# Router and experts of a two-layer transformer: select products ahead of the overflow loop, a shorter overflow body, one more pass in the experts' loop, and extra matmuls while tokens are routed

## The chip, the core and the metric

The kernel runs on one NeuronCore of a Trainium2 chip. The core has a matrix engine (TensorE, PE in the rows), a vector engine (VectorE, DVE), a scalar engine (ScalarE, ACT), GpSimd (POOL) and SyncE (SP). They run their own instruction streams and wait for each other on semaphores. Weights and tokens come from device memory by DMA. The metric is the device time of one execution in microseconds, the median over the runs.

## What is computed

Four layers work on 512 rows of width 1024, in float32. The first two (`hybrid_layer`) are attention layers of three kinds. The last two (`second_block`, DEPTH = 2) are an attention followed by a mixture of 32 experts, and the change is all in the latter. In its first layer 256 context rows are carried along, so 768 rows are routed there and 512 in its second:

```python
p_grp = softmax(h @ w_group + b_group); grp = argmax(p_grp)       # 4 groups
lg = (h @ w_router + b_router)[grp]                               # 8 experts of that group
p_in, e_in = top_k(softmax(lg), 2)                                # 2 experts for each row
wts = p_top * p_in / sum(p_in)
y   = (silu(xe @ w_gate[e]) * (xe @ w_up[e])) @ w_down[e]         # for each expert e and its rows xe
out = segment_sum(y * wts)                                        # rows back in order
x   = x + gt_f * out
```

## The kernel before

A plan written in Python (`make_plan`) makes one list of steps. Each engine walks the same list and issues its own part of each step, so the order on an engine is the order of the list. TR, SC and PJ are the three pairs of PSUM banks; `tr_free`, `sc_free` and `pj_free` count their releases and `tr_full`, `sc_full` and `pj_full` their results.

**Routing.** Behind the attention each tile t of 128 rows (six in the first of the two layers, four in the second) goes through `wo` (L1020, output projection), `fin_turn` (eight transposes, L1015), `scored` (L1161, router products), `logits` (L1167), `ranks` (L1172, L1178; position of each row within its expert) and `slots` (L1184, row numbers of each expert's slots). VectorE finds the two experts of each row in between. GpSimd then gathers the rows of an expert (at most CAP = 96) by an indirect DMA, and `turn_x` (L1236) transposes them.

**Experts.** For expert r, `gate_up` and `gate_up_rest` (L1250, L1260) make the two products of the hidden layer; SiLU and copy (`hidden`, ScalarE) and the product of both (VectorE) give the hidden rows; `turn_hidden` (L1270) transposes them; `down` (L1283, L1291) makes the output rows, which VectorE writes to YR (`rows`). `step(r)` is in this order: gate_up(r+1), turn_hidden(r), gate_up_rest(r+1), turn_x(r+2), down(r). Step 0 stands alone, steps 1 to 28 are a hardware loop (L1321) of 14 passes with two steps in a pass, and steps 29, 30 and 31 are written out behind it.

**The last two experts.** The output rows of experts 0 to 29 go to memory, and those that a tile needs are gathered back (`gather_near`) and added by VectorE (`near_sum`). For the last two experts and the first tiles (NEAR = 2 tiles in the first layer, 4 in the second) the rows stay on the core: `select(t, g)` (L1030) multiplies a selection matrix SLOTTOK[g] (transposed at L1333) with YR[g], for g = 0, 1, into bank t of SC. VectorE adds the bank to the tile in the step `combine`, and `combine_end` normalises it.

**The overflow loop.** An expert with over 96 rows has its further rows worked out in a loop over groups of three blocks (OVER_GROUP), five groups in the first layer and four in the second. On every engine it reads a count, and each pass begins with a test of it:

```python
count = pe.value_load(OVI[0:1, MAX_OVER:MAX_OVER + 1], ...)   # L1348
with pe.Fori(0, over_groups(s.l)) as i:                       # L1349
    with pe.If(j < count):                                    # L1351, passes over the body
        for b in range(OVER_GROUP):                           # L1353, written out three times
```

No weights are loaded for it in the profiled execution: the page has 34 + 30 loads of a gate matrix, which are the 2 x 32 experts, so the body is passed over each time.

**Order around it.** TensorE issues select(0, 0), goes through the loop, and issues the remaining select products in the steps `combine`. VectorE does near_sum of tile 0, the rows of expert 31, near_sum of tile 1, then its own loop, and then the combine steps. Behind the first layer, `fin_turn` of tile 0 and the projection of the next layer (`qkv`, L1201) follow on TensorE; the projection of tile t waits until ScalarE has copied the transposed rows, and in the middle of it the next tile is transposed.

## Time and profile before

| | us |
|---|---|
| runs | 2999.82, 2997.36, 2999.81; median 2999.81 |
| profiled execution | 3009.7 |
| its span (first to last instruction) | 3008.0 |
| TensorE busy in the span | 2817.6 (94%) |
| VectorE, ScalarE, GpSimd busy | 1143.6, 749.9, 324.0 |
| mean granted TensorE clock | 0.968 of full |

The profile is one execution. A matmul of float32 operands is two MATMUL records, each with a weight load (LDWEIGHTS); a transpose is one of each. In a timeline row the number in brackets is the idle time of the engine in front of the row, and the name behind it is what ended that idle time. "issue" is idle time of an engine in which it waited for nothing that the profile names. PEldq and DVEq are the sequencers of TensorE and VectorE, which also run the branches.

### The profile page before, as it was taken

What the parts mean: (1) busy time and instruction counts of PE and PEld (TensorE: products, weight loads), DVE (VectorE), ACT (ScalarE), POOL (GpSimd) and SP (SyncE); (2) the same over time, 40 slices, a digit from 0 to 9 for tenths busy, and PEclk for the clock granted to TensorE, in tenths of its full rate; (3) what the DMA queues carried; (4) which work ended last, traced back from release to release, by engine and by line L of the source; (5) the groups of instructions that cost most, each with busy time, mean ns of one, the idle gap of its engine ahead of it and who ended that gap; (6) DMA issues with size and microseconds to landing.
All of it is one profiled execution on the core that took longest, in us unless ns stands there. A gap on an engine that the chain in (4) does not pass through costs nothing. (4 is left out here: it accounts for less than half of the span.)

```text
span 3008.0 us, 64877 instructions
## 1 busy us (share of the span) xinstructions
PE 2817.6 (94%) x27041; PEld 1647.7 (55%) x27041; DVE 1143.6 (38%) x2779; ACT 749.9 (25%) x1580; POOL 324.0 (11%) x580
## 2 busy tenths in 40 slices
PE   8999999999889999998999999879999799999994
PEld 4444655444654456545666666534565566666662
DVE  2572753572744245454112211353443522112213
ACT  1111531111542156511111111142664111111111
POOL 2000520000520000011100010120000100100001
PEclk9999999999989999998999999989999899999997
DMA  7112643212743100346999999941003699999992
GB/s 267 68 56 84 236 149 105 74 56 84 248 149 124 56 2 2 128 160 254 398 398 403 403 402 395 348 145 64 1 2 120 238 389 402 402 397 405 402 363 84
DMA packets 155293, 636.36 MB, mean 212 GB/s; under 512 B 19712, under 2 KB 24320, under 8 KB 138736
## 3 DMA queue, kind: packets, MB, share of 16 engines
q1 hardware_dynamic: 114624, 517.59, 44.4%
q0 software_dynamic: 40496, 116.39, 11.3%
q8 instruction: 118, 1.93, 0.3%
q14 instruction: 55, 0.45, 0.0%
HBM read 581.91 MB, written 52.00 MB: 211 GB/s over the span
## 5 line engine op out<-in xcount | busy, mean ns | idle before, releaser
L1052 PE MATMUL PJ<-WR,XT 128*128 128x512 f32 (+2 forms) x1152 | 478.0, 571 | 5.7 <-ACT XT L140 3.3
L140 ACT ACTIVATE PT<-TR 128x512 f32<-128x512 f32 (+3 forms) x384 | 178.0, 494 | 904.4 <-PE TR L1270 734.8
L1052 PEld LDWEIGHTS PJ<-WR,XT 128*128 128x128 f32 x1152 | 216.7, 192 | 245.8 <-issue 218.6
L140 DVE TENSOR_TENSOR PR<-G 128x384 f32<-128x384 f32 x64 | 35.7, 558 | 745.3 <-ACT G L140 744.8
L1020 PE MATMUL PJ<-WR,XT 128*128 128x512 f32 x576 | 258.5, 605 | 1.8 <-ACT XT L140 1.4
L1250 PE MATMUL SC<-QK,XT 128*64 128x256 f32 x2112 | 243.5, 384 | 0.0
L140 DVE TENSOR_REDUCE SM<-SC 128x1 f32<-128x768 f32 (+6 forms) x208 | 173.7, 835 | 169.6 <-PE SC L1093 163.0
L1201 PE MATMUL PJ<-WR,XT 128*128 128x512 f32 x512 | 228.7, 599 | 6.1 <-issue 6.1
L1250 PE MATMUL SC<-WR,XT 128*64 128x256 f32 x1984 | 226.2, 381 | 0.0
L1093 PE MATMUL SC<-QK 64*128 64x512 f32 (+7 forms) x512 | 189.3, 534 | 10.8 <-ACT PR L140 10.8
L1250 PEld LDWEIGHTS SC<-QK,XT 128*64 128x64 f32 x2112 | 149.9, 138 | 85.9 <-issue 15.3
L140 ACT ACTIVATE PR<-SC,SM 128x256 f32<-128x256 f32 (+5 forms) x288 | 187.8, 670 | 34.8 <-DVE SM L140 25.6
L1250 PEld LDWEIGHTS SC<-WR,XT 128*64 128x64 f32 x1984 | 139.8, 137 | 79.6 <-issue 12.3
L1020 PEld LDWEIGHTS PJ<-WR,XT 128*128 128x128 f32 x576 | 109.7, 194 | 132.4 <-issue 130.2
L140 ACT ACTIVATE XT<-TR 128x384 f32<-128x384 f32 (+1 forms) x200 | 98.1, 528 | 334.5 <-PE TR L1236 233.8
L1116 PE MATMUL PJ<-V,PT 128*64 128x65 f32 (+1 forms) x3904 | 169.4, 233 | 0.9 <-DVE XS L140 0.8
L1201 PEld LDWEIGHTS PJ<-WR,XT 128*128 128x128 f32 x512 | 95.9, 193 | 114.4 <-issue 114.4
L1106 PE MATMUL TR<-KF,PR 128*128 128x128 f32 x976 | 150.0, 283 | 8.5 <-DVE PR L140 7.8
L1116 PEld LDWEIGHTS PJ<-V,PT 128*64 128x64 f32 x3904 | 137.1, 138 | 36.2 <-issue 34.7
L140 ACT ACTIVATE QK<-TR 128x512 f32<-128x512 f32 (+4 forms) x100 | 54.5, 561 | 380.5 <-PE TR L1060 274.0
L1106 PEld LDWEIGHTS TR<-KF,PR 128*128 128x128 f32 x976 | 106.5, 143 | 66.4 <-ACT PR L140 46.0
L2651 POOL DMA_DIRECT2D y_rows<-XT x62 | 33.3, 537 | 957.0 <-DVE XT L140 951.1
(243 smaller groups left out, 3349.0 us busy)
## 6 DMA issues: line engine op xcount, KB each, us to landing
QK<-in_w_gate_dram SPq DMA_DIRECT2D x34, 2048.0 KB, 9.6
WR<-in_w_down_dram SPq DMA_DIRECT2D x34, 2048.0 KB, 15.8
QK<-in_w_up_dram SPq DMA_DIRECT2D x32, 2048.0 KB, 14.5
WR<-in_w_up_dram SPq DMA_DIRECT2D x32, 2048.0 KB, 14.5
WR<-in_w_gate_dram SPq DMA_DIRECT2D x30, 2048.0 KB, 9.6
QK<-in_w_down_dram SPq DMA_DIRECT2D x30, 2048.0 KB, 16.0
WR<-in_w_ada_dram SPq DMA_DIRECT2D x24, 2048.0 KB, 7.9
WR<-in_w_in_dram SPq DMA_DIRECT2D x14, 2048.0 KB, 7.7
```

What stands on the lines that cost most here:

```text
L140: return lambda *a, **k: Signal(make(*a, **k), self)
L1020: m = mm(dst[:, 0:n], rows[:, c, :], w[:, c, 0:n], start=c == 0, stop=c == DC - 1)
L1052: m = mm(bank[:, 0:n], XT1[:, c, s.t * P:(s.t + 1) * P], w[:, c, 0:n], start=c == 0, stop=c == DC - 1)
L1093: m = mm(SC[:, u.sc % 2, col:col + n], lhsT, rhs, start=all(p[0] // 512 != bank for p in ps[:k]), stop=all(p[0] // 512 != bank for p in ps ...
L1106: m = turn(bank[:, b * P:(b + 1) * P], src, identF)
L1116: m = mm(bank[r:r + HALF_ROWS, col:col + n], PT[:, o + r:o + r + HALF_ROWS], v, start=b == 0, stop=b == len(vs) - 1)
L1201: m = mm(bank, rows[:, c, :], w[:, c, :], start=c == 0, stop=c == DC - 1)
L1250: mm(bank[CAP_A * h:CAP_A * (h + 1), k * 512:k * 512 + 256], XET[par][:, c, 0:CAP_A], w[:, c, 256 * h:256 * (h + 1)], start=c == 0, stop=c ...
L2651: dma(dst, YR[r % 2][0:CAP]).then_inc(y_stored[r % 2], 16)
```

## The change

It has four parts.

1. `select` of tiles 0 and 1 is issued wholly ahead of the overflow loop; the loop's own products now go to PJ, since SC holds the results. VectorE's near_sum of tile 1 moves from ahead of its loop to behind the combine of tile 0 (in the first layer its first operation, `choices_sum`, directly behind that).
2. In the overflow loop the three blocks of a group are a hardware loop on all engines in place of three copies of the body.
3. The experts' loop takes 15 passes in place of 14 on TensorE and ScalarE. Steps 29 and 30 are in it; only turn_hidden(31) and down(31) stand behind it, with the transposes of the selection matrices between them. A loop pass also transposes expert r + 2, so there is now a gather and a turn_x for a 33rd "expert" (the index column of the first overflow block), whose rows nobody reads.
4. A new step `busy(count)` issues `count` products of the identity with a constant matrix of 512 columns into a bank of PJ, with no reader. There are 2 + 1 + 3 + 6 = 12 of them in the routing of each layer, and 2 behind the first `fin_turn` of the first layer.

```diff
@@ make_plan: routing of the last tiles
         t = moe_tiles - 1
+        def busy(count, s=None):
+            add("busy", count=count, pj=n["pj"], s=s)
+        busy(2)
         route_step("logits", t - 1)
+        busy(1)
         add("fin_turn", f=fins[t], tr=take("tr", 2))
...
         route_step("slots", t - 2)
+        busy(3)
         route_step("ranks", t)
         route_step("slots", t - 1)
         route_step("slots", t)
+        busy(6)
         add("route", ...)
...
             xt_ready[0] = add("fin_turn", f=combines[0], tr=take("tr", 2)).tr[-1]
+            busy(2)
             front(2)
@@ tensor engine
+                elif s.kind == "busy":
+                    if s.s is not None:
+                        pe.wait_ge(std_in, s.s.sd)
+                    bank = pj_slot(s.pj)
+                    for _ in range(s.count):
+                        mm(bank, identF, KF[:, 0:512], start=True, stop=True)
...
-                    with pe.Fori(0, EXPERTS // 2 - 2) as i:
+                    with pe.Fori(0, EXPERTS // 2 - 1) as i:
                         for r in (1, 2):
                             step(lambda a, b: i * a + b, r)
-                    step(once, EXPERTS - 3)
-                    gate_up(once, EXPERTS - 1)
-                    turn_hidden(once, EXPERTS - 2)
-                    gate_up_rest(once, EXPERTS - 1)
+                    turn_hidden(once, EXPERTS - 1)
                     pe.wait_ge(sel_ready, s.l + 1)
                     for g in range(2):
-                        use = T0 + 3 * EXPERTS - 1 + g
+                        use = s.tr[g - 2]
...
-                    down(once, EXPERTS - 2)
-                    step(once, EXPERTS - 1, ahead=False)
+                    down(once, EXPERTS - 1)
...
                     select(s, 0, 0)
-                    o = over[s.l]
                     pe.wait_ge(pj_free, s.pj[-1] + 1)
+                    select(s, 0, 1).then_inc(sc_full, 1)
                     pe.wait_ge(sc_free, s.sc[EXPERTS - 1] + 1)
+                    select(s, 1, 0)
+                    select(s, 1, 1).then_inc(sc_full, 1)
+                    o, near = over[s.l], s.near
                     pe.wait_ge(over_ready, s.l + 1)
...
                         with pe.If(j < count):
-                            for b in range(OVER_GROUP):
+                            with pe.Fori(0, OVER_GROUP) as b:
...
-                elif s.kind == "combine" and s.near:
-                    m, t = s.moe, s.t
-                    if t == 0:
-                        select(m, 0, 1).then_inc(sc_full, 1)
-                    else:
-                        if t >= 2:
-                            pe.wait_ge(sc_free, m.sc[EXPERTS + t - 2] + 1)
-                        select(m, t, 0)
-                        select(m, t, 1).then_inc(sc_full, 1)
+                elif s.kind == "combine" and s.near and s.t >= 2:
+                    pe.wait_ge(sc_free, s.moe.sc[EXPERTS + s.t - 2] + 1)
+                    select(s.moe, s.t, 0)
+                    select(s.moe, s.t, 1).then_inc(sc_full, 1)
@@ vector engine
+            def choices_sum(f):
+                y0, y1 = NEAR_Y[f.t]
+                dve.wait_ge(y_scaled, f.scaled)
+                now(STT(y0, y1, W12[:, 6 + f.t:7 + f.t], y0, ALU.mult, ALU.add))
...
                 elif s.kind == "combine" and s.near:
-                    if s.t >= 2:
+                    if s.t:
                         near_sum(s)
...
                         TT(x, x, NEAR_Y[s.t][1], ALU.add).then_inc(std_in, 1)
+                        if s.t == 0:
+                            choices_sum(s.moe.f[1])
...
-                    near_sum(s.f[1])
+                    dve.wait_ge(xs_loaded[s.f[1].fin % 2], 16 * s.f[1].load)
@@ GpSimd
+                    gather(once, EXPERTS, slice(EXPERTS, EXPERTS + 1))
                     store(once, EXPERTS - 3, ...)
```

ScalarE's experts' loop and the four other overflow loops (SP, ScalarE, VectorE, GpSimd) change in the same way as TensorE's.

The instructions of TensorE behind the experts' loop of the first layer, before. Waits stand in brackets; "xN" is N calls; L1250 and L1260 are gate_up and its rest, L1270 turn_hidden:

```order
L1321 REGISTER_ALU
L1321 COMPARE_AND_BRANCH
L1250 MATMUL SC<-WR,XT 64x256 [waits w_loaded2,sc_free,tr_free]
L1250 MATMUL SC<-WR,XT 64x256 x15
L1250 MATMUL SC<-QK,XT 64x256 [waits w_loaded3]
L1250 MATMUL SC<-QK,XT 64x256 x15
L1270 MATMUL TR<-KF,PR 128x128 [waits tr_free,hid_ready]
L1270 MATMUL TR<-KF,PR 128x128 x2
L1260 MATMUL SC<-WR,XT 32x128 x32
```

And of the change, where L1286 is turn_hidden, L1346 the transposes of the selection matrices, L1299 and L1307 down:

```order
L1337 REGISTER_ALU
L1337 COMPARE_AND_BRANCH
L1286 MATMUL TR<-KF,PR 128x128 [waits tr_free,hid_ready]
L1286 MATMUL TR<-KF,PR 128x128 x2
L1346 MATMUL TR<-KF,PT 96x128 [waits tr_free,sel_ready]
L1346 MATMUL TR<-KF,PT 96x128
L1346 MATMUL TR<-KF,PT 96x128 [waits tr_free]
L1346 MATMUL TR<-KF,PT 96x128
L1299 MATMUL PJ<-WR,PT 64x512 [waits pj_free,tr_free,w_loaded2]
```

Before, gate_up of expert 30 follows the branch back (L1321). Now gate_up of experts 30 and 31 is in the loop, and the last turn_hidden follows the branch (L1337).

TensorE from the last expert's down to the overflow loop of the first layer, before. L1030 is select, L1348 reads the count, L1351 is the test:

```order
L1283 MATMUL PJ<-WR,PT 64x512 [waits pj_free,tr_free,w_loaded2]
L1283 MATMUL PJ<-WR,PT 64x512 x7
L1291 MATMUL PJ<-WR,PT 32x256 [waits pj_free]
L1291 MATMUL PJ<-WR,PT 32x256 x15
L1030 MATMUL SC<-XT,PR 128x512 [waits pj_free,tr_free,sc_free]
L1030 MATMUL SC<-XT,PR 128x512
L1348 TENSOR_LOAD SMI [waits over_ready,sc_free,pj_free]
L1348 ISA x2
L1349 UNCONDITIONAL_BRANCH
L1349 ISA
L1351 COMPARE_AND_BRANCH
```

And of the change (L1039 is select, L1362 reads the count, L1365 is the test):

```order
L1307 MATMUL PJ<-WR,PT 32x256 [waits pj_free]
L1307 MATMUL PJ<-WR,PT 32x256 x15
L1039 MATMUL SC<-XT,PR 128x512 [waits pj_free,tr_free,sc_free]
L1039 MATMUL SC<-XT,PR 128x512
L1039 MATMUL SC<-XT,PR 128x512 [waits pj_free]
L1039 MATMUL SC<-XT,PR 128x512
L1039 MATMUL SC<-XT,PR 128x512 [waits sc_free]
L1039 MATMUL SC<-XT,PR 128x512 x3
L1362 TENSOR_LOAD SMI [waits over_ready]
L1362 ISA x2
L1363 UNCONDITIONAL_BRANCH
L1363 ISA
```

Eight products of select stand ahead of the read of the count in place of two, and the read itself waits for `over_ready` alone.

TensorE at the end of the routing of the first layer, before (L1172 and L1178 ranks, L1184 slots, L1236 the transposes of the gathered rows):

```order
L1184 MATMUL SC<-V 96x32 [waits slot_ready]
L1184 MATMUL SC<-V 96x32
L1172 MATMUL SC<-SEL,KB 128x32 [waits rank_read,mask_ready]
L1172 MATMUL SC<-SEL,KB 128x32 x5
L1178 MATMUL SC<-SEL,KB 128x32 [waits rank_read]
L1178 MATMUL SC<-SEL,KB 128x32 x5
L1184 MATMUL SC<-V 96x32 [waits slot_ready]
L1184 MATMUL SC<-V 96x32
L1184 MATMUL SC<-V 96x32 [waits slot_ready]
L1184 MATMUL SC<-V 96x32
L1236 MATMUL TR<-KF,XT 128x96 [waits tr_free,xe_loaded0]
```

And of the change (L1188 and L1194 ranks, L1200 slots, L1179 the products without a reader, L1252 the transposes):

```order
L1179 MATMUL PJ<-KF 128x512 x2
L1188 MATMUL SC<-SEL,KB 128x32 [waits rank_read,mask_ready]
L1188 MATMUL SC<-SEL,KB 128x32 x5
L1194 MATMUL SC<-SEL,KB 128x32 [waits rank_read]
L1194 MATMUL SC<-SEL,KB 128x32 x5
L1200 MATMUL SC<-V 96x32 [waits slot_ready]
L1200 MATMUL SC<-V 96x32
L1200 MATMUL SC<-V 96x32 [waits slot_ready]
L1200 MATMUL SC<-V 96x32
L1179 MATMUL PJ<-KF 128x512 [waits pj_free]
L1179 MATMUL PJ<-KF 128x512 x5
L1252 MATMUL TR<-KF,XT 128x96 [waits tr_free,xe_loaded0]
```

Products without a reader stand in front of the last ranks, and six of them in front of the transposes that wait for the gather.

## Rows read from the trace of the kernel before

**Rows 1.** Timeline, TensorE, end of first layer's experts: start, us, operation, idle before.
```profile
1947.10 1.98 PE L1030 MATMUL SC<-XT,PR 96*128 96x512 f32 x4
1959.93 8.48 PE L1030 MATMUL SC<-XT,PR 96*128 96x512 f32 x12 [10.85 <-issue]
...
1976.35 5.38 PE L1201 MATMUL PJ<-WR,XT 128*128 128x512 f32 x8 [6.12 <-issue]
...
1992.86 1.45 PE L1015 MATMUL TR<-KF,G 128*128 128x128 f32 x8 [3.38 <-DVE G L140]
...
2005.21 1.09 PE L1015 MATMUL TR<-KF,G 128*128 128x128 f32 x8 [1.83 <-DVE G L140]
```

**Rows 2.** Operations of one source line (L1351), first and second layer.
```profile
L1351 PEldq COMPARE_BRANCH  x5: 221/221/6727, 1949.9 to 1959.4; - x5
...
L1351 PEldq COMPARE_BRANCH  x4: 221/1994/7158, 2959.1 to 2972.1; - x4
```

**Rows 3.** The same view of L1321, the branch back of the experts' loop.
```profile
L1321 PEldq COMPARE_BRANCH  x28: 76/208/233, 1442.2 to 2905.4; - x28
```

**Rows 4.** Timeline, VectorE and ScalarE, end of the first layer's experts.
```profile
1946.57 1.39 DVE L140 COPY XT<-PJ 64x512 f32<-64x512 f32 x2
...
1963.82 1.23 DVE L140 TENSOR_TENSOR V<-SC,BC 128x1024 f32<-128x1024 f32 x1 [12.15 <-PE SC L1030]
...
1970.50 1.23 DVE L140 TENSOR_TENSOR XS<-XS,TMP 128x1024 f32<-128x1024 f32 x1 [0.16 <-DVE TMP L140]
...
1973.35 2.90 ACT L140 ACTIVATE XT<-TR,SM 128x128 f32<-128x128 f32 x8
```

**Rows 5.** Timeline, TensorE and VectorE, end of the second layer.
```profile
2958.22 1.28 DVE L140 SCALAR_TENSOR_TENSOR XS<-STG,SM,XS 128x1024 f32<-128x1024 f32 x1
...
2972.66 14.17 PE L1030 MATMUL SC<-XT,PR 96*128 96x512 f32 x28 [15.23 <-issue]
...
2980.06 1.22 DVE L140 TENSOR_TENSOR XS<-XS,SC 128x1024 f32<-128x1024 f32 x1 [2.31 <-PE SC L1030]
...
2994.43 1.28 DVE L140 SCALAR_TENSOR_TENSOR G<-G,SM,BC 128x1024 f32<-128x1024 f32 x1
```

**Rows 6.** Operations of line L2368, the test in the overflow loop of VectorE, second layer.
```profile
L2368 DVEq COMPARE_BRANCH  x4: 63/63/69, 2961.7 to 2964.2; - x4
```

**Rows 7.** Timeline, TensorE, behind the experts' loop, first and second layer.
```profile
1928.16 1.88 PE L1260 MATMUL SC<-QK,XT 128*32 128x128 f32 x52
...
1934.45 0.64 PE L1333 MATMUL TR<-KF,PT 128*96 128x128 f32 x4
...
2917.84 1.13 PE L1236 MATMUL TR<-KF,XT 96*128 96x96 f32 x8
...
2924.34 3.67 PE L1250 MATMUL SC<-QK,XT 128*64 128x256 f32 x32
...
2931.88 2.01 PE L1260 MATMUL SC<-QK,XT 128*32 128x128 f32 x53
...
2942.36 1.08 PE L1333 MATMUL TR<-KF,PT 128*96 128x128 f32 x8
...
2950.00 3.65 PE L1283 MATMUL PJ<-WR,PT 128*64 128x512 f32 x16 [0.63 <-issue]
```

**Rows 8.** Timeline, TensorE, while tokens are routed, first and second layer.
```profile
1339.19 7.11 PE L1020 MATMUL PJ<-WR,XT 128*128 128x512 f32 x16
...
1371.48 1.54 PE L1236 MATMUL TR<-KF,XT 96*128 96x96 f32 x8 [5.90 <-DMA XT<-h_rows,SMI]
...
1374.95 9.13 PE L1250 MATMUL SC<-QK,XT 128*64 128x256 f32 x64
1384.02 3.70 PE L1260 MATMUL SC<-QK,XT 128*32 128x128 f32 x128
...
2380.62 8.07 PE L1250 MATMUL SC<-QK,XT 128*64 128x256 f32 x64
```

**Rows 9.** Busy time in one stretch by engine (PE, PEld, DVE, ACT, POOL), PEclk, DMA share, GB/s.
```profile
1352.00:1363.00 11.00, 6.26 (x43) 5.09 (x43) 9.41 (x46) 1.83 (x4) 1.06 (x2) 0.50 0.37 147
```

More of the change, by code:

```diff
@@ L489, in make_plan @@
         bc = take("bc")[0]
-        moe = add("moe", l=l, bc=bc, last=last, tiles=moe_tiles, xe0=[16 * 16 * l] * 2, tr=take("tr", 4 + 3 * EXPERTS - 2),
+        moe = add("moe", l=l, bc=bc, last=last, tiles=moe_tiles, xe0=[16 * 17 * l, 16 * 16 * l], tr=take("tr", 4 + 3 * EXPERTS),
                   sc=take("sc", EXPERTS + NEAR[l]), pj=take("pj", 2 * EXPERTS), base=base, order=order,
@@ L1351, in _ @@
                         with pe.If(j < count):
-                            for b in range(OVER_GROUP):
+                            with pe.Fori(0, OVER_GROUP) as b:
                                 pe.wait_ge(o["x"], j * 16 + 16 * b + 16)
@@ L1620, in _ @@
                     hidden(once, 1)
-                    with act.Fori(0, EXPERTS // 2 - 2) as i:
+                    with act.Fori(0, EXPERTS // 2 - 1) as i:
                         for r in (1, 2):
@@ L1626, in _ @@
                             hidden(lin, r + 1)
-                    hidden_turned(once, EXPERTS - 3)
-                    x_in(once, EXPERTS - 1)
-                    hidden(once, EXPERTS - 2)
-                    hidden_turned(once, EXPERTS - 2)
+                    hidden_turned(once, EXPERTS - 1)
                     for g in range(2):
-                        use = T0 + 3 * EXPERTS - 1 + g
+                        use = s.tr[g - 2]
                         act.wait_ge(tr_full, use + 1)
                         copy(SLOTTOK[g][0:CAP, 0:s.near * P], TR[0:CAP, use % 2, 0:s.near * P]).then_inc(tr_free, 1)
-                    hidden(once, EXPERTS - 1)
-                    hidden_turned(once, EXPERTS - 1)
-                    a.count[tr_free.name] += 6 * (EXPERTS // 2 - 3)
-                    a.count[sc_free.name] += 2 * (EXPERTS // 2 - 3) + s.near
+                    a.count[tr_free.name] += 6 * (EXPERTS // 2 - 2)
+                    a.count[sc_free.name] += 2 * (EXPERTS // 2 - 2) + s.near
                     a.latest = (tr_free, a.count[tr_free.name])
@@ L1659, in _ @@
                         with act.If(j < count):
-                            for b in range(OVER_GROUP):
+                            with act.Fori(0, OVER_GROUP) as b:
                                 act.wait_ge(o["turned"], j + b + 2)
@@ L1771, in near_sum @@
                 else:
-                    dve.wait_ge(y_scaled, f.scaled)
-                    now(STT(y0, y1, W12[:, 6 + f.t:7 + f.t], y0, ALU.mult, ALU.add))
+                    if f.t == 0:
+                        choices_sum(f)
                     now(TT(y0, y0, BC[:, 0:D], ALU.mult))
@@ L2363, in _ @@
                     dve.wait_ge(over_ready, s.l + 1)
-                    side, near = s.sc[EXPERTS - 1] % 2, s.near
+                    near = s.near
                     count = dve.value_load(OVI[0:1, MAX_OVER:MAX_OVER + 1], min_val=0, max_val=MAX_OVER)
@@ L2368, in _ @@
                         with dve.If(j < count):
-                            for b in range(OVER_GROUP):
+                            with dve.Fori(0, OVER_GROUP) as b:
                                 dve.wait_ge(o["ix"], j * 2 + 2 * b + 2)
@@ L2393, in _ @@
                                     TT(x, x, rows_, ALU.add).then_inc(o["added"], 1)
+                                dve.wait_ge(o["added"], j * near + near * b + near + 1)
                     v.latest = (pj_free, v.count[pj_free.name])
@@ L2687, in _ @@
                         with pool.If(j < count):
-                            for b in range(OVER_GROUP):
+                            with pool.Fori(0, OVER_GROUP) as b:
                                 pool.wait_ge(pj_full, s.pj[-1] + 1)
                                 for k in range(2):
-                                    pool.wait_ge(xe_loaded[k], s.xe0[k] + 16 * 16)
+                                    pool.wait_ge(xe_loaded[k], s.xe0[k] + 16 * (17 - k))
                                 pool.wait_ge(o["turned"], j + b + 1)
```

18 lines of the change are left out of this document (8 added, 10 removed).

## The prediction

> **What bounds the kernel now.** I read the waits of TensorE first, then the timelines around them. TensorE is busy for 94% of the span, and while the experts run it has no idle time at all. So the change can win only where TensorE idles or runs slowly: behind the experts' loops and in the routing. The largest waits of the trace stand at `select`: 10.85 us in the first layer of experts [rows 1] and 15.23 us in the second [rows 5]. Both are "issue", so no engine and no DMA is named. The sequencer's own rows name it. The test at L1351 passes over the overflow body. It takes 221 ns as a rule, but 6,727 ns once in the first layer and up to 7,158 ns in the second, where the median of four is 1,994 ns, so that a second one must be near 1,994 x 2 - 221 = 3,767 ns [rows 2]. The misses are thus 6.5 us and 3.5 + 6.9 = 10.4 us of the two waits. The same instruction on VectorE takes no such time: its four tests start within 2.5 us [rows 6].
>
> The count of instructions fits a fetch of code as the cause. A select call of two products is four MATMUL records with four weight loads, so a product is 4 instructions, a transpose 2. One copy of the overflow body has 14 transposes and 28 products in the first layer (140 instructions) and 16 and 32 in the second (160). Three copies are 420 and 480, and the branch leaps over all of them.
>
> The Trainium skill ("Runtime: NRT & Kernel Launch", Instruction fetch mechanics) says that code comes in blocks of 256 instructions, and that a taken branch to a target outside a window of two blocks waits for a DMA. By that rule a leap of 420 or 480 can miss and one of 140 or 160 cannot; the misses in rows 2 agree. But the rule also has the branch back over the experts' two steps (about 1,000 instructions) miss in every pass, and the trace has it at 76 to 233 ns in all 28 [rows 3]. So backward leaps go by the trace, and the page's rule for them is a rival below.
>
> **The change part by part.** The sum is made against the profiled execution (3009.7 us, span 3008.0), which is 9.9 us above the median of 2999.81.
>
> *Select and the overflow loop, second layer.* Now select(0, 0) is done at 2957.43 (2972.66 - 15.23), and TensorE then waits out its loop until 2972.66; VectorE has finished the rows of expert 31 at 2958.22 and near_sum of tile 1 two operations of 1.29 us later, at 2960.8. Its sum of tile 1 starts at 2980.06, which puts that of tile 0 at 2976.53 (2.31 of idle time and 1.22 of work earlier), and its last operation ends at 2995.71 [rows 5]. After the change TensorE goes on at 2958.2 with three more select calls of 1.98 us [rows 1], up to 2964.2. Its sequencer needs about 1 us to read the count and 4 x 0.8 us for the passes (the tests and what stands between them: the last starts at 1959.4, 3.6 passes after the miss ended at 1956.6 [rows 2]), all beside those products. VectorE passes its loop from 2958.2 to about 2961.9 (its tests ran from 2961.7 to 2964.2 after a start at 2960.8, so 3.7 us [rows 6]). Then come the sum of tile 0 (1.22), near_sum of tile 1 (2.6), the sum of tile 1 (1.22), and after these the same list as before: from 2967.1, where the trace has 2981.3 (2980.06 plus 1.22). The rest is bound by VectorE and takes 14.4 us from there, so the last operation ends near 2981.5 in place of 2995.7. That is 14.2 us. Select of tile 2 begins at 2964.2 and is done at 2968.2 (at half clock 2972.1), and VectorE wants it at 2971.3: hidden, or 1 us late.
>
> *The same in the first layer.* VectorE writes the last rows by 1947.96 [rows 4], passes its loop by 1951.7, and finds select of tile 0 ready at 1951.1. It starts the sum of tile 0 at 1951.8 in place of 1963.82. From there to ScalarE's copy for the next projection (1973.35) the trace has 9.5 us [rows 4]. To these come two operations of near_sum that now stand in between (2 x 1.25; the third hides in the wait for the norm), so the copy starts at 1963.9, 9.5 us early. ScalarE copies the selection matrices before it scales the rows of tile 0, where it did so earlier before, which costs up to 0.8 us. I take 8.8. Next, TensorE waits 3.38 us for tile 2 where later tiles wait 1.83, and runs the transposes at 1.45 in place of 1.09 us [rows 1]; with the gathers of the far tiles, which wait for the last select of tile 1, started 13 us earlier (1955.0 for 1968.4 [rows 1]) that excess goes, and so does part of the slow stretch behind it. Bounds 0 and 5, I take 3.3: the steady cadence of 1.83 us is a loop between the engines and stays. Sum 12.1. The two products without a reader cost nothing, since TensorE idles there for over 6 us both ways. They do not bridge it, and the 5.38 us of the first projection stay.
>
> *The experts' loop.* Behind its last pass TensorE runs written-out code, and gate_up_rest of expert 31 takes 6.29 us in the first layer (1928.16 to 1934.45) and 10.48 in the second (2931.88 to 2942.36) [rows 7], against 3.70 in full flow [rows 8]. The losses, 2.6 and 6.8 us, are split in pieces of "issue". After the change this code is inside the loop, and the 6 + 96 instructions of the last turn_hidden and down follow. The 0.63 us in front of the last down [rows 7] is covered by the transposes of the selection matrices, worth 0.6. The extra turn_x costs 1.1 us in each layer [rows 7]; its gather waits on nothing that TensorE needs, as store(29) behind it on GpSimd waits for rows that come 20 us later. Net gain 2.1 and 6.3 us. Bounds: nothing of the stalls gone (-0.5 each) or all.
>
> *Products without a reader.* One is two records of 7.11 / 16 = 0.44 us, 0.89 us. From 1352 to 1363 the granted clock is 0.50 (1.2 GHz) with TensorE busy 6.26 of 11 us [rows 9]. That time is not TensorE's to win: VectorE is busy 9.41 of these 11 us with finding experts. Behind it, the clock does count. The last ranks and slots are worth 0.45, turn_x 1.54 against 1.13 (0.4), and gate_up(0) 9.13 and 8.07 [rows 8] against 2 x 3.65 [rows 7] (1.85 and 0.75). So 2.7 and 1.6 us if the clock holds. The six products take 5.3 us at full clock and stand in a wait of 5.90 us [rows 8], where they are free; the other six (5.3 us together) stand in the stage of rows 9, where TensorE idles 4.7 of 11 us, and in the wait just ahead of it. At half clock the six take 10.7 and push turn_x back by 4.8.
>
> *Sum.* First layer 2.7 + 2.1 + 12.1 = 16.9; second 1.6 + 6.3 + 14.2 = 22.1; together 39.0 us. Against the profiled execution that is 2970.7, against the median 2960.8. The 9.9 us between the two may sit in just those stalls of code fetch, in which case the unprofiled runs gain less. I count a quarter of it, 2.5 us: 36.5 us, **2963 us**.
>
> **Rivals.**
>
> *The stalls behind the experts' loop are not code fetch.* GpSimd issues the gathers for the first tiles at that time. If these slow TensorE wherever it is, 9.4 us stay: 2972. For it: the stall comes in small pieces. Against: every pass of the loop has two gathers and TensorE no idle time.
>
> *The test in the overflow loop still misses.* A block's edge may lie badly, and up to 6.5 and 10.4 us remain. In the first layer this hides: the loop would end at about 1960.4, ScalarE needs the transposes by 1963.9. In the second select(2) starts near 2973 in place of 2964.2 and ends at 2977 to 2981, where VectorE wants it at 2971.3: 6 to 9 us lost, 2971.
>
> *The clock stays low.* The clock falls in spite of the added products, and the six take up to 10.7 us: 4.8 us later per layer at turn_x and nothing of the 4.3 won, together 13.9 us: 2977. For it: the last slots and ranks are products of 32 columns. Against: the added products fill most of the idle time that the stage has.
>
> *The longer experts' loop misses in its branch back.* The code has moved, and if the body (about 1,000 instructions, as before) no longer lies in the store at once, each of the 28 taken branches would cost 3.5 to 6.9 us as in rows 2, 98 to 193 us: 3061 to 3156. It turns the change into a loss from 36.5 / 28 = 1.3 us a branch. This is also what the page's window of two blocks would give, against rows 3, where the same body never missed.
>
> **How the numbers follow.** Forecast 0.63, with its own range 2954 to 2972 (the first layer's 3.3 and 8.8 us, the profile's 9.9 us); stalls not fetch 0.12; test still misses 0.10; clock 0.09; branch back 0.03; and 0.03 for gains that are all given back at the next wait, within 0.2% (about what a measurement of this kernel tells from no change). Faster 0.94, same 0.03, slower 0.03. The range 2951 to 2980 leaves out the branch back and the tails.
>
> **What would show it.** In the changed profile: no wait of "issue" over 1 us at select; all nine tests near 0.22 us; select of tiles 0 and 1 without a gap; gate_up_rest at 3.7 us up to the last; VectorE's first sum of the second layer about 4 us behind its last rows in place of 18; a granted clock of 1.0 between the last `wo` and gate_up(0), with the six products ending before the gather lands. It would be wrong if the tests still miss where VectorE waits for them, if the six products run past the gather, or if the branch back at L1337 shows microseconds.

## The result, and the profile after

In the first comparison the kernel before took 2999.82 us (median of 5) and the changed one 2983.16 us (5 runs, 2975.46 to 2987.54): 16.7 us less. The ratio of changed to before was 0.9934, with a 95% interval of 0.9915 to 0.9953. Two more comparisons, beside the experiments, gave 0.9914 [0.9898, 0.9931] and 0.9932 [0.9916, 0.9949]. The medians differ by 16.7, 25.4 and 20.7 us, on average 20.9; the mean ratio, 0.9927, would be 22 us of 3000. The forecast was 36.5 us, with a range down to 20. So the direction was right, and the size too large by 11 to 20 us.

The table is worked out from first starts of rows in the timelines. "Routing" runs from the last product of `wo` (the row of 16 records) to gate_up(0), "loop" from there to gate_up_rest(31), "exit" from there to the first select, "first end" from there to the last `wo` of the next layer, "end" from the last layer's first select to the end.

| kernel, profile | up to last wo | routing 1 | loop 1 | exit 1 | first end | routing 2 | loop 2 | exit 2 | end |
|---|---|---|---|---|---|---|---|---|---|
| before, 1st | 1339.2 | 35.8 | 553.2 | 18.9 | 398.0 | 35.5 | 551.3 | 23.6 | 52.5 |
| before, 2nd (b1) | 1337.3 | 35.7 | 553.0 | 18.9 | 396.9 | 35.6 | 551.7 | 23.7 | 45.5 |
| before, 3rd (b2) | 1343.1 | 35.8 | 552.8 | 19.1 | 396.6 | 35.4 | 551.8 | 23.9 | 45.4 |
| before, 4th (b3) | 1337.6 | 35.7 | 552.8 | 19.1 | 396.5 | 35.5 | 551.8 | 23.9 | 47.8 |
| after, 1st | 1339.9 | 36.4 | 552.7 | 19.8 | 385.5 | 35.8 | 551.7 | 24.2 | 36.9 |
| after, 2nd (a1) | 1335.9 | 36.1 | 553.1 | 19.8 | 385.9 | 35.8 | 551.3 | 24.2 | 37.0 |
| after, 3rd (a2) | 1338.1 | 35.1 | 551.2 | 19.8 | 385.5 | 36.1 | 551.3 | 24.2 | 36.9 |

Only two stretches became shorter: the first end by 11.4 us (397.0 to 385.6 on average) and the last by 8.5 to 15.5. The two exits, for which 8.4 us were forecast, are longer by 0.8 and 0.4. Routing and the loop behind it, for which 4.3 us were forecast, are together 0.5 us shorter in the first layer and 0.2 longer in the second.

The end of the first layer, TensorE in the profile after; these rows answer to [rows 1]:

```profile
1948.70 7.14 PE L1039 MATMUL SC<-XT,PR 96*128 96x512 f32 x16
1957.90 1.09 PE L1024 MATMUL TR<-KF,G 128*128 128x128 f32 x8 [2.06 <-DVE G L140]
1958.83 3.26 PE L1179 MATMUL PJ<-KF 128*128 128x512 f32 x4
1967.62 6.26 PE L1217 MATMUL PJ<-WR,XT 128*128 128x512 f32 x8 [5.54 <-issue]
...
1983.38 1.09 PE L1024 MATMUL TR<-KF,G 128*128 128x128 f32 x8 [1.75 <-DVE G L140]
```

All four select calls are one row, and the wait of 10.85 us is gone. The first projection starts 18.9 us behind the first select, where it was 29.3. It is slower than before (6.26 against 5.38 us), and the two products without a reader in front of it ran at half speed too (four records in 3.26 us; four took 1.96 at full clock). The wait of 3.38 us is now 1.75, as forecast.

The test in TensorE's overflow loop (L1365 now) in all nine passes of both layers, for [rows 2]:

```profile
L1365 PEldq COMPARE_BRANCH  x9: 221/221/381, 1951.6 to 2951.6; - x9
```

No test is over 381 ns. The end of the second layer, TensorE and then VectorE, for [rows 5]:

```profile
2945.88 1.98 PE L1039 MATMUL SC<-XT,PR 96*128 96x512 f32 x4
2948.19 12.28 PE L1039 MATMUL SC<-XT,PR 96*128 96x512 f32 x28 [0.33 <-DVE XT L140]
```

```profile
2946.40 1.73 DVE L140 TENSOR_TENSOR XT<-PJ,BC 32x256 f32<-32x256 f32 x4 [0.83 <-PE PJ L1307]
2950.28 1.22 DVE L140 TENSOR_TENSOR XS<-XS,SC 128x1024 f32<-128x1024 f32 x1 [2.15 <-PE SC L1039]
...
2969.22 1.28 DVE L140 SCALAR_TENSOR_TENSOR G<-G,SM,BC 128x1024 f32<-128x1024 f32 x1
```

VectorE's first sum starts 2.15 us after its last rows, where it was 18.3 (2958.22 to 2976.53).

Behind the experts' loop, in the second layer, for [rows 7]:

```profile
2921.72 2.00 PE L1276 MATMUL SC<-QK,XT 128*32 128x128 f32 x51
2924.01 0.43 PE L1276 MATMUL SC<-QK,XT 128*32 128x128 f32 x6 [0.29 <-issue]
2924.74 0.44 PE L1276 MATMUL SC<-QK,XT 128*32 128x128 f32 x5 [0.30 <-issue]
2926.17 0.27 PE L1276 MATMUL SC<-QK,XT 128*32 128x128 f32 x1 [0.99 <-issue]
...
2927.60 0.43 PE L1276 MATMUL SC<-WR,XT 128*32 128x128 f32 x4 [1.00 <-issue]
2928.32 0.27 PE L1276 MATMUL SC<-WR,XT 128*32 128x128 f32 x1 [0.30 <-issue]
2929.04 3.24 PE L1276 MATMUL SC<-WR,XT 128*32 128x128 f32 x57 [0.45 <-issue]
2932.21 1.13 PE L1252 MATMUL TR<-KF,XT 96*128 96x96 f32 x8
```

It still takes 10.49 us, in the same pieces as before. The gaps make up 3.3 us of it. The clock fell with them: it was granted at 0.71 from 2927.72 to 2929.72 and at 0.50 for the 2 us behind that, and the last 57 records took 3.24 us. Yet this code now stands inside the loop, whose last branch comes 5 us later. That alone speaks against the forecast's reading. What GpSimd issues in the same microseconds are the six gathers for the first tiles, one every 1.25 us:

```profile
2920.58 0.99 POOL L2497 DMA_INDIRECT V<-y_rows,SMI  x1 [3.70 <-DMA y_rows<-XT]
2921.88 0.96 POOL L2497 DMA_INDIRECT V<-y_rows,SMI  x1 [0.30 <-issue]
...
2926.87 0.94 POOL L2497 DMA_INDIRECT BC<-y_rows,SMI  x1 [0.30 <-issue]
```

The branch itself, for [rows 3]:

```profile
L1337 PEldq COMPARE_BRANCH  x30: 76/208/241, 1442.9 to 2937.4; - x30
```

The routing in the first layer, for [rows 8]:

```profile
1352.89 1.09 PE L1024 MATMUL TR<-KF,G 128*128 128x128 f32 x8 [0.76 <-DVE G L140]
...
1359.79 5.47 PE L1179 MATMUL PJ<-KF 128*128 128x512 f32 x6
1365.05 0.36 PE L1188 MATMUL SC<-SEL,KB 128*128 128x32 bf16 x6
...
1376.26 8.42 PE L1266 MATMUL SC<-QK,XT 128*64 128x256 f32 x64
```

The clock held at first (transposes 1.09 us, before 1.97) and fell later. The six records in the middle took 5.47 us, ran past the moment at which VectorE was ready, and gate_up(0) took 8.42 us. The clock fell twice: at about 1358, and again when gate_up(0) began (0.50 from 1376 to 1378). The granted clock of 1352 to 1363 rose from 0.50 [rows 9] to 0.79:

```profile
1352.00:1363.00 11.00, 7.37 (x48) 4.97 (x48) 9.37 (x43) 1.72 (x4) 1.05 (x2) 0.79 0.42 168
...
1354.00:1358.00 4.00, 1.62 (x24) 1.31 (x24) 3.39 (x17) 1.38 (x4) 0.18 (x1) 1.00 0.72 277
1358.00:1362.00 4.00, 3.52 (x14) 2.46 (x15) 3.42 (x17) 0.00 (x0) 0.00 (x0) 0.55 0.02 4
```

### The profile page after: what moved, and what is told of

Read it like the earlier page. It is cut to its first block and busy times, and to the rows that moved or that the text cites. A ratio compares the mean times of both kernels' runs of the same rounds, so it can differ in the third digit from the quotient of the medians.

```text
span 2982.9 us, 65090 instructions
## 1 busy us (share of the span) xinstructions
PE 2838.0 (95%) x27109; PEld 1652.6 (55%) x27109; DVE 1143.5 (38%) x2779; ACT 750.6 (25%) x1584; POOL 323.5 (11%) x584
## 5 line engine op out<-in xcount | busy, mean ns | idle before, releaser
L140 DVE TENSOR_TENSOR PR<-G 128x384 f32<-128x384 f32 x64 | 35.7, 558 | 745.8 <-ACT G L140 745.4
L140 ACT ACTIVATE PR<-SC,SM 128x256 f32<-128x256 f32 (+5 forms) x288 | 187.6, 669 | 32.9 <-DVE SM L140 23.9
```

The lines of the kernel that those rows point to most:

```text
L140: return lambda *a, **k: Signal(make(*a, **k), self)
```

## The experiments

Theory G: TensorE's stall behind the loop comes from GpSimd's gathers for the first tiles, which follow one another at that time. Theory F: it is a fetch of code. For the gap between profile and median, theory V: the fetches missed at the test vary from execution to execution. Theory N: they do not.

**The changed kernel again (a1, a2).** No edit.

> The changed kernel once more, beside the experiments of this group, so that they are compared with it and not with a number from another chip. The first comparison gave a ratio of 0.9934, 2983.16 us. Theory V (the code fetches of the profiled execution of before, 6.5 and 10.4 us, are shorter in other executions): the profiled execution of this kernel, which has no such fetch, lies within 3 us of its own median again. Theory N (the 9.9 us of the profiled execution of before are accident of that execution, in any part of the program): a repeated profile of this kernel may lie as far from its median too.

> The changed kernel beside the two below on one chip. Expected from its two former comparisons: a ratio of 0.991 to 0.9935 and a profile with gate_up_rest(31) at 6.3 and 10.5 us once more.

2978.05 us (ratio 0.9914) and 2982.08 us (0.9932). The profiled execution is 2.8 us over the median in a1, 1.4 over it in the first comparison and 2.0 under it in a2. Theory V expected 3 us at most, but N allows this too, so these runs do not decide between them. The part up to the last `wo`, which is the same code in all versions, took from 1333.0 to 1343.1 us in the 17 profiles. So a single profile of this program is good to some 5 us, whatever is changed.

**No products without a reader (e1).**

```
-        busy(2)
         route_step("logits", t - 1)
-        busy(1)
...
-        busy(3)
         route_step("ranks", t)
         route_step("slots", t - 1)
         route_step("slots", t)
-        busy(6)
...
-            busy(2)
             front(2)
```

> The changed kernel without any product that has no reader. Theory A (they cost as much as they give: the six records of the fourth group ran 1.2 us past the moment at which VectorE was ready for ranks, and gate_up(0) was no faster than before): within 1.5 us of the changed kernel, and gate_up(0) with its rest takes the same 12.2 us. Theory B (the forecast's: a held clock is worth 2.7 + 1.6 us): 3 to 5 us slower than the changed kernel. Theory C (they only delay): 2 to 3 us faster.

2983.71 us, 0.9931 [0.9913, 0.9949]. Against a1 of the same chip the median is 5.7 us slower. The two profiles are 5.8 us apart, and 4.0 of these lie in the part up to the last `wo`, where nothing differs. Behind that part e1 is 1.8 to 4.7 us longer than the three profiles of the changed kernel. Its routings took 35.6 and 36.0 us, in the first layer 0.5 and 0.8 us less than in a1 and the first; gate_up(0) then took 8.89 and 9.57 us, where the first profile of the changed kernel had 8.42 and 8.19. So theory A (within 1.5 us, and gate_up(0) as long as with the products) isn't confirmed, C (2 to 3 us faster) has neither the profile nor the median for it, and B isn't shown: the intervals overlap, and a gain of 3 us from these products is neither shown nor excluded. Where the clock fell for a shorter time, as in a2 and e3 (2 of 12 profiles with the products), the first layer's routing and loop took 586.3 and 586.0 us together, some 3 us less than in the first profile and a1 (589.1 and 589.2). In e3:

```profile
1352.74 4.31 PE L1179 MATMUL PJ<-KF 128*128 128x512 f32 x6
...
1367.80 7.13 PE L1266 MATMUL SC<-QK,XT 128*64 128x256 f32 x64
```

The instructions and their distances are the same as in the changed kernel's routing, so these alone don't decide what the clock does there.

**Gathers for the first tiles later (e2).**

```
+                    pool.wait_ge(sc_full, s.sc[EXPERTS - 1] + 1)
                     for f in s.f[0:min(s.near, 3)]:
                         gather_near(f)
```

> GpSimd starts the gathers of the rows for the first tiles only when gate_up_rest of the last expert is done. Theory G (TensorE loses 2.7 us in the first layer and 6.8 in the second because these gathers follow one another at that time): gate_up_rest(31) takes 3.7 us in both layers; the same idle pieces of 0.3 and 1.0 us come later, in down(30) or down(31), or nowhere. Theory F (something at this place of the code, a fetch or the end of the loop): gate_up_rest(31) still takes 6.4 and 10.5 us, with the gathers behind it. Under G with the stall gone for good the profiled span is 9 us shorter; with the stall moved it is the same. If the unprofiled time doesn't move although the profiled span does, the stall belongs to the profiler.

2977.15 us, 0.9906 [0.989, 0.9922]. TensorE in the second layer:

```profile
2920.85 1.96 PE L1276 MATMUL SC<-QK,XT 128*32 128x128 f32 x64
2922.62 1.93 PE L1276 MATMUL SC<-WR,XT 128*32 128x128 f32 x64
...
2934.62 0.94 PE L1346 MATMUL TR<-KF,PT 128*96 128x128 f32 x4 [2.64 <-ACT PT L140]
```

gate_up_rest(31) is at full speed, so the stall is the gathers', and F is out. TensorE ran down(30) without a gap (2925.55 to 2931.06) beside the first five of six gathers, which were issued from 2925.42 to 2932.67. The stall went elsewhere: ScalarE and VectorE, whose inputs were ready at 2931.5 and 2931.1, both started at 2934.0:

```profile
2934.02 1.73 DVE L140 TENSOR_TENSOR XT<-PJ,BC 32x256 f32<-32x256 f32 x4 [3.39 <-remote]
...
2934.07 0.49 ACT L140 ACTIVATE PT<-TR 128x384 f32<-128x384 f32 x1 [7.17 <-remote]
```

The exits are 17.1 and 21.4 us in place of 19.8 and 24.2, but the whole span is that of a1 (2978.9 against 2979.0 us): here the stall is moved more than removed. The first end lost 2 us. There VectorE waited 3.29 us for ScalarE to scale the late rows of tile 0, wrote the last rows of expert 31 later, and TensorE's select waited 1.62 us for them.

**The experts' loop at 14 passes (e3).** The edit puts back what the change removed.

```
-                    with pe.Fori(0, EXPERTS // 2 - 1) as i:
+                    with pe.Fori(0, EXPERTS // 2 - 2) as i:
...
+                    step(once, EXPERTS - 3)
+                    gate_up(once, EXPERTS - 1)
+                    turn_hidden(once, EXPERTS - 2)
+                    gate_up_rest(once, EXPERTS - 1)
```

> The experts' loop back at 14 passes, with the last steps written out behind it; all the rest as in the changed kernel. Theory F (a fetch of code behind the loop, now hidden): slower, and the gap of 0.6 us before the last down is back. Theory G (the 15th pass took nothing away and costs the transposes of an expert that isn't there, 1.13 us in each layer): 1 to 2 us faster than the changed kernel, with gate_up_rest(31) at 6.4 and 10.5 us as in both kernels.

2979.27 us, 0.9917 [0.9902, 0.9933]; a1 had 0.9914. The exits are 19.0 and 23.6 us, 0.8 and 0.6 less. gate_up_rest(31) keeps its stall with 14 passes, so G again: the 15th pass brought nothing. It costs 1.4 us in the profile, which the median can't resolve; in its one profile the first end was also 3.5 us longer (389.1), with no cause in the edit.

**Three copies of the overflow body (e5).** The edit is the same on all five engines. Products ahead stay.

```
-                            with pe.Fori(0, OVER_GROUP) as b:
+                            for b in range(OVER_GROUP):
```

> The changed kernel with three copies of the overflow body in every engine again, in place of the loop. Theory M (the missed fetches at the test are what the shorter body takes away; the products ahead hide them in the first layer, while VectorE wants select of tile 2 before TensorE is through in the second): tests of 3 to 7 us are back in the profile; the first layer loses 0 to 1 us, the second 6 to 9 us: 6 to 9 us slower than the changed kernel. Theory V (such fetches are shorter outside of the profiled execution): the profile shows them and the other runs are under 4 us slower.

2986.69 us, 0.9947 [0.9932, 0.9963]. The misses are back, one in each layer:

```profile
L1365 PEldq COMPARE_BRANCH  x5: 221/221/6872, 1951.6 to 1961.4; - x5
...
L1365 PEldq COMPARE_BRANCH  x4: 221/221/3432, 2952.3 to 2957.9; - x4
```

With the products ahead the profile hides that of 3.4 us in the second layer (end 37.2 us, 36.9 without it), and the first end is 3.3 us longer: TensorE comes out of its loop 6.03 us after the select products, at 1961.98, and only then transposes tile 0. In the changed kernel it waited 2.06 us there. M had it the other way round, with 0 to 1 us in the first layer and 6 to 9 in the second, so its split isn't confirmed. The ratio is 0.0020 above the mean of the changed kernel's three, about 6 us, and its interval overlaps two of theirs. So with the products ahead the short body brings about 6 us, not safely told from none. M's 6 to 9 us fit this total, V's under 4 us do not.

**Products behind the loop (e8).** The loop stays short.

```
-                    select(s, 0, 1).then_inc(sc_full, 1)
-                    pe.wait_ge(sc_free, s.sc[EXPERTS - 1] + 1)
-                    select(s, 1, 0)
-                    select(s, 1, 1).then_inc(sc_full, 1)
...
                                 pe.wait_ge(o["free"], j + b + 2)
+                    select(s, 0, 1).then_inc(sc_full, 1)
+                    pe.wait_ge(sc_free, s.sc[EXPERTS - 1] + 1)
+                    select(s, 1, 0)
+                    select(s, 1, 1).then_inc(sc_full, 1)
```

> The changed kernel with select (0, 1), (1, 0) and (1, 1) behind the overflow loop again, which stays short. What the products ahead are worth by themselves once no fetch is missed: VectorE passes its loop in 3.7 us, TensorE in about 4.2 us, so VectorE waits 1 to 2.5 us more for its first sum in each layer. Theory L (the gain of both ends is nearly all the fetches'): 2 to 5 us slower than the changed kernel. Rival (a TensorE that idles for 4 us in front of the products runs them at half clock): 6 to 10 us slower.

2996.2 us (11 runs), 0.9977 [0.9967, 0.9988]. First end 392.3 us against 385.6 (6.7 more), end 42.4 against 36.9 (5.5 more): 12.2 us, and by the ratios some 15 (0.9977 against 0.9927 on average). L had 2 to 5, the rival 6 to 10: both were too low, and the rival's mechanism, slower products behind the wait, is what the rows show. TensorE, first layer:

```profile
1947.20 1.98 PE L1039 MATMUL SC<-XT,PR 96*128 96x512 f32 x4
1953.77 7.42 PE L1039 MATMUL SC<-XT,PR 96*128 96x512 f32 x12 [4.59 <-issue]
1963.06 1.09 PE L1024 MATMUL TR<-KF,G 128*128 128x128 f32 x8 [1.87 <-DVE G L140]
```

The loop without a miss takes 4.59 us, and the twelve records behind it 7.42 where e2's took 5.42. In the second layer the wait is 4.27 us and the 28 records behind it take 13.97 in place of 12.28. These four numbers, 4.59 + 2.00 + 4.27 + 1.69, add up to 12.6 us, near the 12.2 of the two ends. They follow from the place of the products alone, and they are the largest part of the gain. Against the kernel before, e8 keeps some 7 us (0.9977), which go to the other parts together.

**Plain transfers for the gathers (e6, e6b).** The same number and size; which rows are chosen is left out.

```
-                    pool.indirect_dma_start(NEAR_Y[f.t][j], None, YD[:, :],
-                                            bass.IndirectOffsetOnAxis(ap=DEST[:, 6 * j + f.t:6 * j + f.t + 1], axis=0)
-                                            ).then_inc(near_in[f.t], 16)
+                    dma(NEAR_Y[f.t][j], YD[(2 * f.t + j) * P:(2 * f.t + j + 1) * P, :]).then_inc(near_in[f.t], 16)
```

> The rows of the first tiles' tokens are not chosen: a plain transfer of 128 neighbouring rows stands in place of each of the near gathers, of the same size and at the same time (2 per tile). Theory G (TensorE is held by GpSimd's indirect transfers that follow one another): gate_up_rest of the last expert takes 3.7 us in both layers, and the profiled span is 8 to 9.5 us shorter than that of the changed kernel (2979.0). The runs outside of the profile are shorter by as much if the stall is a stall of the program, and by under 3 us if it is one of the profiler. Theory D (the amount of data moved from and to memory holds TensorE): the stall stays.

> As e6_plain_near (plain transfers of neighbouring rows in place of the near gathers, so the choice of rows is left out), to settle whether TensorE's stall of 2.7 + 6.8 us is there in executions whose trace isn't kept. Its profiled span was 9.5 us shorter than that of the changed kernel, its median 3.0 us. Theory P (the stall is a stall of the program): 7 to 10 us under the median of the changed kernel of this group. Theory R (the profiler makes it, or most of it): 0 to 4 us under it, though the profiled stretches differ by 9 us again.

2975.03 us, 0.9909 [0.9891, 0.9928], and 2972.76 us, 0.9891 [0.9873, 0.9908]. Profiled spans 2969.5 and 2972.1, exits 17.1 and 17.3 us in both, which are 2.7 and 6.9 us less. e6b's median is 9.3 us under that of a2 on the same chip. gate_up_rest(31) in the second layer of e6 has no gap:

```profile
2915.61 1.95 PE L1276 MATMUL SC<-QK,XT 128*32 128x128 f32 x64
2917.38 1.93 PE L1276 MATMUL SC<-WR,XT 128*32 128x128 f32 x64
```

Beside the first 2 us of it 371 GB/s were moved; in the changed kernel the stretches with the gaps had 358 and 266 (2923.72 to 2927.72). So it isn't the bytes that hold TensorE, and the stall is there in ordinary executions as well (P). The 3.0 us between e6 and a1 came from two chips and had suggested otherwise. The plain transfers are also issued faster, six within 3.2 us, so these runs don't tell the indirect kind from the longer issue.

**Each tile's gathers when the last ones have landed (e7).**

```
+                        if f.t:
+                            pool.wait_ge(near_in[f.t - 1], 32 * (s.l + 1))
                         gather_near(f)
```

> Each tile's two near gathers start only when those of the tile before have landed, so that two and no more are under way at a time. In the first group the stall began some 3.4 us after the first gather, when the third was issued. Theory T (up to two indirect transfers under way do no harm, as one in each pass of the loop doesn't): gate_up_rest(31) at 3.7 us in both layers, no new wait (each tile needs 6 us for its transfers, the last is wanted 15 us later): 7 to 9 us faster than the changed kernel. Theory I (any of them costs 1 to 1.5 us whenever TensorE issues fast): the pieces of idle time spread but stay, 0 to 2 us faster.

2975.58 us, 0.9906 [0.9888, 0.9925]. Exits 18.6 and 17.7 us: 1.2 and 6.5 us less. Two gathers in a row cost 0.4 to 1.5 us, six cost 6.9. That is theory T, but for the first pair. The exits give 7.7 us, where the median has 2.5 against a1 and 6.5 against a2, both of other chips; its interval overlaps that of the changed kernel.

**Both corrections (e9), and tile 3's gathers held back too (e11).** e9 is the edits of e3 and e7 together. e11 adds this to it:

```
                         pool.wait_ge(near_begun, 1)
+                        pool.wait_ge(near_in[2], 32)
                         gather_near(s.f[3])
```

> The changed kernel with both corrections that the runs suggest: the experts' loop at 14 passes (no transposes for an expert that isn't there) and each tile's near gathers started when those of the tile before have landed. By the profiles of the two alone: 1.5 us from the loop, 7.7 us from the gathers, so a profiled span near 2970 and, if stalls of the profile count in full in other executions, a median near 2969; if they count by a third, as the medians of the two alone suggest, near 2975.

> As e9_both (14 passes, each tile's near gathers when those of the tile before have landed), with tile 3's two gathers in the second layer now held back in the same way. In e9_both they came straight behind tile 2's, four in a row, and VectorE wrote its last rows 2.3 us late and its first sum began 3.9 us after them. Theory G (a third and fourth gather in a row hold whatever engine works then, TensorE or VectorE): no wait over 1 us between VectorE's last rows, the last stretch 37 in place of 41.5 us, a span near 2969 and a median of 2968 to 2973. Rival (tile 3's rows now come too late for VectorE): a wait on a DMA ahead of tile 3's sum, and no gain over e9_both.

e9: 2974.82 us, 0.9901 [0.9884, 0.9917]; its exits are 16.5 and 17.0 us, but its end is 41.2 us. GpSimd and then VectorE in e9:

```profile
2928.03 1.17 POOL L2506 DMA_INDIRECT V<-y_rows,SMI  x1 [4.63 <-DMA TMP<-y_rows,SMI]
2929.51 1.02 POOL L2506 DMA_INDIRECT BC<-y_rows,SMI  x1 [0.30 <-issue]
2930.83 0.94 POOL L2506 DMA_INDIRECT V<-y_rows,SMI  x1 [0.30 <-issue]
2932.07 0.94 POOL L2506 DMA_INDIRECT V<-y_rows,SMI  x1 [0.30 <-issue]
```

```profile
2933.78 1.73 DVE L140 TENSOR_TENSOR XT<-PJ,BC 32x256 f32<-32x256 f32 x4 [2.25 <-remote]
2939.45 1.22 DVE L140 TENSOR_TENSOR XS<-XS,SC 128x1024 f32<-128x1024 f32 x1 [3.94 <-PE SC L1039]
```

Four gathers in a row, and now VectorE is late twice by 1.8 us. In e11 the last pair waits for the third to land:

```profile
2934.11 1.73 DVE L140 TENSOR_TENSOR XT<-PJ,BC 32x256 f32<-32x256 f32 x4 [0.45 <-PE PJ L1307]
2937.99 1.22 DVE L140 TENSOR_TENSOR XS<-XS,SC 128x1024 f32<-128x1024 f32 x1 [2.15 <-PE SC L1039]
```

The end is 36.8 us again, and no wait on a DMA stands ahead of VectorE's sums, so the rival of e11 did not come. e11 takes 2972.11 us, 0.9893 [0.9879, 0.9907], within what was expected. It is the fastest version that computes everything, some 10 us under the changed kernel by the mean ratio; its interval overlaps that of a1.

**The kernel before, profiled three more times (b1, b2, b3).** No edit.

> The kernel before, profiled once more. In its first profile, 9.9 us over the median, the tests that pass over the overflow body lost 6.5 us in the first layer and 10.4 us in the second. Theory V (the fetch is what varies): other sizes now, the sum nearer to 7 us, and a time nearer to 3000. Theory N (they are the same in each execution, and the 9.9 us lay elsewhere, as in the first 1345 us, where nine profiles of other versions of this code already took 1339.5 to 1347.1 us for the same work): again 6 to 7 us and 9 to 11 us.

> The kernel before, a third profile. The first had misses at the test of 6.5 us (first layer) and 10.4 us (second), the second 7.1 and 3.2 us, and the stretch from the last down to the end took 52.8 and 45.8 us. If the second layer's misses vary between one and two, this profile falls by one of these two (45 to 47, or 52 to 54 us), and the time follows; if the first profile was a single accident, it has 45 to 47.

> The kernel before, a fourth profile; expectation as for the third.

2999.99, 3005.57 and 3002.31 us. The tests of L1351, second layer, in b1, then b2, then b3:

```profile
L1351 PEldq COMPARE_BRANCH  x4: 221/221/3388, 2956.4 to 2962.0; - x4
```

```profile
L1351 PEldq COMPARE_BRANCH  x4: 221/221/3359, 2962.1 to 2967.6; - x4
```

```profile
L1351 PEldq COMPARE_BRANCH  x4: 221/221/4619, 2956.7 to 2963.4; - x4
```

One miss in place of the two of [rows 2]: a loss of 3.2, 3.1 and 4.4 us for 10.4. The first layer's is the same in all four (6.5 to 7.1 us). That is V, for the second layer only.

## Why the prediction was wrong

*Products ahead and the short loop: right.* 12.1 us were forecast for the first end, and 12.5 were found against the first profile of before (11.4 against all four). For the last 14.2 were forecast and 15.5 found against that profile. The forecast gave VectorE 3.7 us between its last rows and its first sum; the profile has 2.15 us in the second layer, which accounts for that difference. The split of the waits into misses and the rest held as well: it left 4.3 and 4.8 us, and e8, whose tests don't miss, waits 4.59 and 4.27. That the products without a reader would not bridge the wait in front of the projection was right too.

*The profile's 9.9 us: mis-sized.* I took a quarter of them, 2.5 us, as fetches that other executions don't have. The second miss was nearly all of it: the end took 52.5 us in that profile and 46.2 on average in the other three. The part up to the last `wo` was usual. The term should have been about 6.3 us, so 3.8 us were forecast too much. The failing step of this term is that the misses of one profile were added as if every execution had them, although their second was already odd (one test of 1,994 x 2 - 221 ns beside one of 7,158).

*The experts' loop: failed.* The largest error. The step that failed is the reading of the "issue" gaps in gate_up_rest(31) as fetches of written-out code. "After the change this code is inside the loop" was true, and nothing followed from it. 8.4 us were forecast, and the exits became 0.8 and 0.4 us longer (19.0 to 19.8, 23.8 to 24.2): 9.6 us. The stall is that of GpSimd's gathers (e2, e6, e7), and it is still there with the code inside the loop (10.49 us). The rival had this, with the right engine, at 0.12. My argument against it, that two gathers stand in every pass without harm, compared gathers 17 us apart (an expert's time in the loop) with four and six that follow each other at 1.25 us.

*Products without a reader: failed.* 4.3 us were forecast on the condition that the clock holds, and 0.3 came (0.5 less 0.2). That is before against after; against e1, which lacks only these products, it may be more, and the runs don't settle it. The clock fell all the same in the first layer, only later, from 1358 on, and once more at gate_up(0), which took 8.42 us in place of 9.13, and 8.19 in place of 8.07 in the second layer; the six records in the middle then lasted 5.47 us in place of 2.7 and pushed ranks back by 1.2 us. That is the clock rival, at 0.09, in its first half. Its 4.8 us for the last twelve records did not come: those ran at full clock (5.40 us).

*The other rivals* did not come: with the short body no test was over 383 ns in any of twelve profiles, and the branch back stayed at 241 ns or less. What the first of them says of the first layer, that a miss hides there, is wrong: e5 lost 3.3 us to one.

Together: 36.5 - 3.8 - 9.6 - 4.0 = 19.1 us, and 20.8 with the 1.7 us that the two ends gave over the forecast. The three comparisons had 20.9 on average. That it comes out so near is in part luck: against the other three profiles of before the first end gained 11.0 us and not 12.5, and the terms differ by up to a microsecond from profile to profile. That the comparisons differ by 9 us among themselves is not explained; the part up to the last `wo` varies by as much in the profiles, and nothing in the change touches it.

## What to carry to other kernels

Before a stall is priced as gone, take a second profile of the same kernel: of two misses that made up 10 us, one was there in every profile and the other in one of four profiles. When an engine idles in pieces while it has all that it needs, look at what the other engines issue in those microseconds, above all runs of indirect transfers; spacing them took two waits and was worth, together with the loop back at 14 passes, about half as much as the whole change (10 us, e11). Work that can stand in front of a loop of tests should stand there even if no test misses, because the wait costs its own length and the clock of the work behind it.

## What the runs showed of the hardware

While GpSimd issued indirect gathers of 128 rows every 1.25 us, other engines stood still, mostly from the third gather on: TensorE in gate_up_rest in pieces of 0.3 and 1.0 us, in another arrangement ScalarE and VectorE for 2.5 to 2.9 us. Two gathers in a row cost 0.4 to 1.5 us, six 6.9, part of which is the clock that fell with the gaps. Plain transfers of the same size every 0.53 us held none. TensorE ran another stage (down) beside five gathers at full speed. Which resource they share isn't shown: the stall struck where TensorE issues 256 short instructions in 3.7 us, and where engines wait for another engine's signal, and no run here separates these.

A test that leaps over about 420 or 480 TensorE instructions missed once per layer in five profiles (3.4 to 7.3 us, and twice in one layer once). A leap over a third of that was never above 383 ns in twelve profiles. No row names the cause; that it is a fetch of code is inferred from the length. This agrees with what the Trainium skill states of fetches in blocks and targets outside of them ("Runtime: NRT & Kernel Launch", Instruction fetch mechanics); its window of two blocks would also have the branch back over the experts' body of about 1,000 instructions miss in every pass, which no profile here shows (76 to 241 ns). The same section gives TensorE a store of 2,048 instructions, which would hold that body; no run here tests its size.
